# A transformer trunk on one core: the products of probabilities and values with v as the stationary operand, and the probabilities divided on GpSimd

## The chip, the cores and the metric

The kernel runs on one core of a Trainium2 chip. The metric is the device time of one execution in microseconds (us); the median of three runs is compared. Engines are named as in the profile: PE (TensorE's matmuls), PEld (its weight loads), DVE (VectorE), ACT (ScalarE), POOL (GpSimd) and SP, which issues most of the DMAs.

## The reference

Two layers over 256 tokens of width 1024. Each has a mixer, then a feed-forward part: dense (width 2816) in layer 0, eight experts with two chosen per token (width 3584) in layer 1. What the change touches is the mixer's attention and what follows it:

```python
scores = jnp.einsum('bnqkgd,bnskd->bnkgqs', qb, kb).astype(jnp.float32) * (HEAD_DIM ** -0.5)
scores = jnp.where(valid[None, :, None, None], scores, NEG_INF)
m = jnp.maximum(jnp.max(scores, axis=-1, keepdims=True), sink_b)
p = jnp.exp(scores - m)
denom = jnp.sum(p, axis=-1, keepdims=True) + jnp.exp(sink_b - m)
probs = (p / denom).astype(v.dtype)
out = jnp.einsum('bnkgqs,bnskd->bnqkgd', probs, vb)
...
y_att = rmsnorm(window_attention(q, k, v, sink), att_out_g)
y_conv = rmsnorm(short_conv(bg, cg, u, conv_w), conv_out_g)
return jnp.concatenate([y_att, y_conv], axis=-1) @ w_out
```

There are 8 query heads of 64 columns over 2 key/value heads (4 query heads share one), and 512 channels of short convolution.

## The kernel before, in words

Every engine has its own hand-written list of instructions; semaphores order them against each other, and each engine takes its list strictly in order. So the order of the work around the change is the order of the calls in `mixer(layer)`, which stands once for PE, once for ACT and once for DVE.

A float32 weight is multiplied as two parts, `hi` (ACT's rounded copy) and `lo` (DVE's remainder), and so is the activation (`act_hi`, `act_lo`); `three` issues the three products. A "piece" is 128 x 1024 of weights: PE takes 12 matmuls of 512 columns for it. The pieces of a mixer are numbered q 0 to 3, kv 4 and 5, c 6 to 9, u 10 to 13, b 14 to 17, out0 18 to 21, out1 22 to 25. `hi` and `lo` are rings of six pieces, so ACT can turn out piece n only when PE is through with piece n - 6.

Between the pieces PE does the attention for two blocks of 128 queries, t = 0 and t = 1. `scores` writes the scores of eight heads into banks 0 to 3. On DVE `masked_scores` adds the mask and takes the maximum, two heads at a time; on ACT `exps` takes the exponentials of them, into the tile `prob`, with their sums. `turn_probs` (PE) transposes the 16 squares of `prob` into the same four banks, `probT_copy` brings them to SBUF (two banks by ACT, two by DVE), and `values` multiplies: for each head and each half of the keys the 128 x 128 square of transposed probabilities is the stationary operand and 64 columns of v are streamed, 16 matmuls of 64 columns for each t. `attended` on DVE multiplies the result by 1/denominator (`denominators`, `rden`) into the tile `att`. PE then transposes `att` (eight squares), ACT and DVE make `act_hi` and `act_lo` of it, and `out_pieces` multiplies by `w_out`: first the two pieces of the convolution's channels (k = 4 to 7), then the two of the attention's (k = 0 to 3), for each half of the output columns. The sum of the attention's squares comes from ACT (`ss_a`), that of the convolution's from a DVE reduction and a matmul with ones (L2001).

Names in rows and in the order: `raw_d` is the memory in which `prob`, `probT`, qkv, qT, kT and zT lie (it holds the dense part's weights later), `y` and `gated` hold the convolution's result and its squares, `silu` the sums of squares, `raw_gu` the raw weights. SP loads them, and the experts' weights only after the router's decision (`order_done`) at the end of layer 1's mixer.

Of the kernel before, what the change touches and what calls it, by code (L numbers as in the profile page):

```python
# [33 lines left out]
P = 128  # L34
# [26 lines left out]
             ("out0", 4, 1, 2), ("out1", 4, 2, 2)]  # L61
# [269 lines left out]
CONSTS = 7  # L331
# [3 lines left out]
def build_trunk(nc, x_d, pos_d, mix_g, w_in, conv_w, sink, att_g, conv_g, w_out, ffn_g, dg, du, dd,  # L335
                router, eg, eu, ed, final_g, out_d):
    ctx = ExitStack()
    with ctx:
# [8 lines left out]
        def sem(name):  # L347
            return ctx.enter_context(nc.semaphore(name))
# [153 lines left out]
        def e_at(s, g):  # L502
# [21 lines left out]
        att = qT.rearrange("p c n -> p (c n)").rearrange("p (t n) -> p t n", t=NT)  # L524
# [4 lines left out]
        sq_sum = silu[:, 0, :]  # L529

# [22 lines left out]
        av_done, att_done, attss_done, attms_done, attstd_done, attn_done = (  # L553
            sem("av_done"), sem("att_done"), sem("attss_done"), sem("attms_done"), sem("attstd_done"), sem("attn_done"))
# [3 lines left out]
        attT_done, mixhi_done, mixlo_done = sem("attT_done"), sem("mixhi_done"), sem("mixlo_done")  # L558
# [74 lines left out]
        w_out_v = w_out.rearrange("l (h p k) n -> l h p k n", h=2, k=4)  # L633
# [10 lines left out]
        def _(sp):  # L644
# [3 lines left out]
            def mixer_loads(layer):  # L648
# [4 lines left out]
                for name, _, buf, _ in MIX_UNITS:  # L653
# [26 lines left out]
            def dense_down(j):  # L680
                if j < 2:

                    sp.wait_ge(mixlo_done, 8)
                else:
                    sp.wait_ge(lo_done, DENSE_BASE + d_first(2 * (j - 2) + 1, DH) + 2)
# [69 lines left out]
        def _(pool):  # L755
# [13 lines left out]
            nc.gpsimd.dma_start(g_att[:, :, :], att_g.rearrange("l (p k) -> p l k", k=4)).then_inc(consts_in, 16)  # L769
# [28 lines left out]
            nc.gpsimd.dma_start(gain_rows[:, :], ffn_g[1].partition_broadcast(P)).then_inc(gain_in, 16)  # L798
            pool.wait_ge(gain_in, 16)
# [5 lines left out]
        def _(act):  # L805
# [64 lines left out]
            def exps(layer, t):  # L870
# [7 lines left out]
                act.wait_ge(sinkd_done, 2 * layer + t + 1)  # L878
                nc.scalar.activation(esink[:, t, :], sinkd[:, t, :], ACT.Exp).then_inc(exp_done, 1)

            def probT_copy(layer, t):
                act.wait_ge(probT_done, 2 * layer + t + 1)
                for b in range(2):
                    copy(probT[:, b * 512:(b + 1) * 512], bank[b][:, :]).then_inc(probT_out_a, 1)

            def mixer(layer):
# [53 lines left out]
                act.wait_ge(yc_done, layer + 1)  # L940
                for k in range(CT):
                    copy(act_hi[:, 4 + k, :], yc[:, k, :], scale=g_conv[:, layer, k:k + 1]).then_inc(mixhi_done, 1)
# [1541 lines left out]
```

## Time and profile before

| | |
|---|---|
| median of 3 runs | 1271.81 us (1270.8 to 1272.67) |
| profiled execution | 1271.47 us, of it the span 1270.0 us |
| instructions | 31539 |
| PE busy | 1241.2 us (98%) |
| DVE busy | 578.2 us (46%) |
| ACT busy | 435.0 us (34%) |
| POOL busy | 11.8 us (1%) |

"Busy" is the time in which an engine has at least one instruction under way. A row of the timeline gives start, duration, engine, line, what is written and read, the shape, and in brackets how long the engine had sat idle before and what ended it. The difference between the starts of two neighbours on one engine is what the first costs that engine; its duration also has a tail that overlaps the next.

### The profile page before, as it was taken

The page shows a single profiled execution, that of the slowest core. Times are in us where ns is not written, and L with a number is a line of the kernel's source. Part 1 is how long each engine was busy: PE and PEld are TensorE (multiplying, and loading weights), DVE is VectorE, ACT ScalarE, POOL GpSimd, SP SyncE. Part 2 cuts the span into 40 slices and gives each one's busy share as a digit, 9 for nine tenths or more (in the row PEclk, how much of TensorE's full clock was granted, in tenths as well). Part 3 has the DMA queues.
Part 4 walks back from the last instruction along what each step waited for, and adds up shares of the span by engine and source line. Part 5 has one row for each costly group of instructions (what it writes and reads, how often), then busy time and mean ns, then how long its engine had stood idle before and what let it go on. Part 6 is the DMA issues. An engine that isn't in the chain of part 4 may idle for free.

```text
span 1270.0 us, 31539 instructions
## 1 busy us (share of the span) xinstructions
PE 1241.2 (98%) x14347; PEld 967.1 (76%) x14347; DVE 578.2 (46%) x940; ACT 435.0 (34%) x674; POOL 11.8 (1%) x35
## 2 busy tenths in 40 slices
PE   7999999999998999999999999999999999999997
PEld 6888888888887777777767778766677778768894
DVE  5785555556686656565765657421100112210003
ACT  7664444445553544454643445200000000000002
POOL 3000000000000000000000000000000000000000
PEclk9999999999998999999999999999999999999999
DMA  9345844165005999999999999999999999999993
GB/s 344 139 168 208 315 161 172 69 234 195 5 1 205 421 420 425 419 421 421 421 425 421 420 421 421 421 423 419 419 416 420 394 396 396 419 419 421 421 421 134
DMA packets 109018, 419.50 MB, mean 330 GB/s; under 512 B 4632, under 2 KB 8768, under 8 KB 100688
## 3 DMA queue, kind: packets, MB, share of 16 engines
q1 hardware_dynamic: 107776, 416.30, 81.0%
q8 instruction: 115, 1.88, 0.5%
q0 software_dynamic: 544, 1.12, 0.3%
q14 instruction: 23, 0.19, 0.0%
q10 hardware_dynamic: 560, 0.01, 0.0%
HBM read 416.37 MB, written 1.05 MB: 329 GB/s over the span
## 4 chain that ended last, share of the span: by engine, by line
PE 87%; DMA 9%; DVE 2%; ACT 1%; issue 0%; SPq 0%; DVEq 0%
PE bank L2236 26%; PE bank L1854 14%; PE bank L1855 13%; PE bank L1856 13%; PE bank L2300 13%; DMA ring<-in_moe_w_down 5%; DMA ring_after<-in_moe_w_down 2%; DMA ring<-in_moe_w_up 2%; PE bank L2165 2%; PE bank L2171 2%; PE bank L1935 1%; PE bank L1913 1%; PE bank L1925 1%; DMA raw_gu<-in_w_in 1%; ACT w_hi L807 0%; PE bank L2250 0%
## 5 line engine op out<-in xcount | busy, mean ns | idle before, releaser
L1646 DVE TENSOR_TENSOR w_lo<-ring,w_hi 128x896 fp32r<-128x896 f32 (+2 forms) x192 | 202.1, 1088 | 78.8 <-ACT w_hi L807 72.9
L2236 PE MATMUL bank<-ring,late_acts 128*32 128x224 f32 x4736 | 234.0, 353 | 0.0
L2236 PEld LDWEIGHTS bank<-ring,late_acts 128*32 128x32 f32 x4736 | 188.9, 110 | 40.9 <-issue 5.0
L807 ACT ACTIVATE w_hi<-ring 128x896 fp32r<-128x896 f32 (+2 forms) x192 | 176.2, 949 | 115.9 <-PE bank L1856 74.0
L1072 ACT ACTIVATE silu_buf<-bank 128x224 f32<-128x224 f32 (+2 forms) x76 | 29.1, 394 | 433.9 <-PE bank L2236 433.9
L1854 PE MATMUL bank<-hi,act_hi 128*128 128x512 f32 (+1 forms) x400 | 154.6, 387 | 3.6 <-DVE act_lo L1227 1.8
L1856 PE MATMUL bank<-hi,act_lo 128*128 128x512 f32 (+1 forms) x400 | 152.5, 381 | 0.0
L1855 PE MATMUL bank<-lo,act_hi 128*128 128x512 f32 (+1 forms) x400 | 152.5, 381 | 0.0
L1202 DVE TENSOR_TENSOR lo<-raw_gu,hi 128x1024 fp32r<-128x1024 f32 x96 | 113.6, 1221 | 41.2 <-ACT hi L807 41.0
L1669 DVE TENSOR_TENSOR silu_buf<-silu_buf,bank 128x224 f32<-128x224 f32 (+2 forms) x76 | 32.0, 434 | 207.3 <-PE bank L2236 186.0
L807 ACT ACTIVATE hi<-raw_gu 128x1024 fp32r<-128x1024 f32 x96 | 97.5, 1060 | 40.6 <-PE bank L1856 36.8
L2236 PE MATMUL bank<-ring,first_acts 128*32 128x224 f32 x2048 | 104.2, 354 | 0.6 <-ACT silu_buf L1072 0.6
L1854 PE MATMUL bank<-w_hi,wide_hi 128*128 128x512 f32 (+1 forms) x256 | 94.9, 371 | 1.0 <-ACT silu_buf L1072 0.9
L1855 PE MATMUL bank<-w_lo,wide_hi 128*128 128x512 f32 (+1 forms) x256 | 94.0, 367 | 0.0
L1856 PE MATMUL bank<-w_hi,wide_lo 128*128 128x512 f32 (+1 forms) x256 | 93.7, 366 | 0.0
L1854 PEld LDWEIGHTS bank<-hi,act_hi 128*128 128x128 f32 x400 | 75.3, 188 | 19.5 <-issue 3.0
L2236 PEld LDWEIGHTS bank<-ring,first_acts 128*32 128x32 f32 x2048 | 63.6, 110 | 33.0 <-issue 5.1
L2300 PE MATMUL bank<-ring,at_buf 128*32 128x256 f32 x1456 | 85.7, 380 | 1.7 <-DMA ring<-in_moe_w_down 1.7
L1856 PEld LDWEIGHTS bank<-hi,act_lo 128*128 128x128 f32 x400 | 75.2, 188 | 14.8
L1855 PEld LDWEIGHTS bank<-lo,act_hi 128*128 128x128 f32 x400 | 75.3, 188 | 13.8
L2300 PEld LDWEIGHTS bank<-ring,at_buf 128*32 128x32 f32 x1456 | 51.5, 110 | 31.8 <-DMA ring<-in_moe_w_down 3.0
L1854 PEld LDWEIGHTS bank<-w_hi,wide_hi 128*128 128x128 f32 x256 | 48.0, 188 | 11.0 <-DVE w_lo L1646 3.2
(249 smaller groups left out, 1340.2 us busy)
## 6 DMA issues: line engine op xcount, KB each, us to landing
ring<-in_moe_w_up SPq DMA_DIRECT2D x59, 1792.0 KB, 20.3
ring<-in_moe_w_gate SPq DMA_DIRECT2D x58, 1792.0 KB, 20.3
ring<-in_moe_w_down SPq DMA_DIRECT2D x53, 1792.0 KB, 20.4
ring_after<-in_moe_w_down SPq DMA_DIRECT2D x11, 1792.0 KB, 19.7
raw_gu<-in_w_in SPq DMA_DIRECT2D x7, 2048.0 KB, 12.4
raw_gu<-in_dense_w_gate SPq DMA_DIRECT2D x5, 2048.0 KB, 7.8
raw_gu<-in_dense_w_up SPq DMA_DIRECT2D x5, 2048.0 KB, 12.7
raw_d<-in_dense_w_down SPq DMA_DIRECT2D x5, 2048.0 KB, 14.5
```

What stands on the lines that cost most here:

```text
L807: return nc.scalar.activation(out, in_, ACT.Copy, **kw)
L1072: nc.scalar.activation(out, gate, ACT.Silu).then_inc(e_silu_done, 1)
L1202: v.tensor_tensor(out, src, h, ALU.subtract).then_inc(lo_done, 1)
L1646: v.tensor_tensor(w_lo[:, n % WP, 0:b - a], flat(u)[:, a:b], w_hi[:, n % WP, 0:b - a], ALU.subtract).then_inc(w_lo_done, 1)
L1669: v.tensor_tensor(gated_e, gated_e, up, ALU.mult).then_inc(e_gated_done, 1)
L1854: mm(out, ah, wh, start=start, stop=False, **kw)
L1855: mm(out, ah, wl, start=False, stop=False, **kw)
L1856: return mm(out, al, wh, start=False, stop=stop, **kw)
L2165: ins = mm(bank[b][:, i * m:(i + 1) * m], xn[:, t, k * P:(k + 1) * P], sel[:, t, 0:m], start=t == 0, stop=t == 1)
L2171: return mm(bank[b][:, :], gselT[0:m, tile, t * P:(t + 1) * P], yt[0:m, tile, c * 512:(c + 1) * 512], start=start, stop=stop)
L2236: ins = mm(bank[b][32 * c:32 * c + 32, 0:n], acts[STEPS[s][0]][:, k, g.col:g.col + 32], w[:, c], start=k == 0, stop=k == KT - 1)
L2300: ins = mm(bank[g.acc][32 * c:32 * c + 32, g.acc_col:g.acc_col + 256], e_at(s, g)[:, 32 * f:32 * f + 32], flat(u)[:, at:at + 256], start=o ...
```

## The change

In `values` the roles are swapped: 64 columns of v are the stationary operand, and the transposed probabilities of the four heads of one key/value head are streamed, 512 columns at once. The two key/value heads write the two halves of the partitions (0 to 63 and 64 to 127) of the same bank. So the result comes out transposed, with channels on partitions, and PE's eight transposes of `att` are gone, as is the tile. Because 1/denominator now belongs to a column, not to a partition, the probabilities are divided before they are turned: POOL multiplies each head's 128 x 256 probabilities by `rden`, 8 instructions for each t and layer, and `turn_probs` waits for them (`probs_done`). The denominators are made in two batches of four heads, between the masks. `act_hi` and `act_lo` are made straight from the bank of `values`, 128 x 128 at a time for each t; the squares' sums go by DVE and two more matmuls with ones. The channels lie on other partitions, so `w_out`'s attention rows and `g_att` are loaded in another order (three DMAs in the place of two for each half of `w_out`; four small ones in the place of one for `g_att`). For t = 1 ACT copies all four banks of turned probabilities. The turn for t = 0 stands one piece later, and the ones-products one piece later.

```diff
 MIX_UNITS = [("q", 4, 0, 1), ("kv", 2, 1, 1), ("c", 4, 2, 1), ("u", 4, 3, 1), ("b", 4, 0, 1),
-             ("out0", 4, 1, 2), ("out1", 4, 2, 2)]
+             ("out0", 4, 1, 3), ("out1", 4, 2, 3)]
...
-                        for h in range(2):
-                            sp.dma_start(unit[buf][:, 4 * h:4 * h + 4, :],
-                                         w_out_v[layer, h, :, :, c * 512:(c + 1) * 512]).then_inc(unit_in[buf], 16)
+                        cc = slice(c * 512, (c + 1) * 512)
+                        sp.dma_start(unit[buf][:, 4:8, :], w_out_conv[layer, :, :, cc]).then_inc(unit_in[buf], 16)
+                        for g in range(NKV):
+                            sp.dma_start(unit[buf][HD * g:HD * g + HD, 0:4, :], w_out_att[layer, g, :, :, cc])\
+                                .then_inc(unit_in[buf], 16)
...
+            for layer in range(2):
+                for t in range(NT):
+                    for n, b in enumerate(SCORE_BANKS):
+                        if n % 2 == 0:
+                            pool.wait_ge(rden_done, 2 * (2 * layer + t) + n // 2 + 1)
+                        for h in (2 * b, 2 * b + 1):
+                            own = prob[:, h * SEQ:(h + 1) * SEQ]
+                            nc.gpsimd.tensor_scalar(own, own, rden[:, t, h:h + 1], None, ALU.mult).then_inc(probs_done, 1)
...
 # ACT
-                for b in range(2):
+                for b in range(2 if t == 0 else 4):
                     copy(probT[:, b * 512:(b + 1) * 512], bank[b][:, :]).then_inc(probT_out_a, 1)
+
+            def attended(layer, t):
+
+                act.wait_ge(av_done, 2 * layer + t + 1)
+                for k in range(4):
+                    copy(act_hi[:, k, t * P:(t + 1) * P], bank[6 + t][:, k * P:(k + 1) * P], scale=g_att[:, layer, k:k + 1])
+                nc.scalar.activation(prob[:, t * 512:(t + 1) * 512], bank[6 + t][:, :], ACT.Square).then_inc(attss_done, 1)
...
 # DVE
+            def denominators(layer, t, c):
+                i = 2 * (2 * layer + t) + c
+                dve.wait_ge(exp_done, 5 * (i + 1))
+                link(v.tensor_tensor(batch(den, t, c), batch(psums, t, c), batch(esink, t, c), ALU.add))
+                v.reciprocal(batch(rden, t, c), batch(den, t, c)).then_inc(rden_done, 1)
...
+                    if n % 2 == 1:
+                        c = n // 2
+                        dve.wait_ge(masked_done, 4 * i + n + 1)
+                        v.tensor_tensor(batch(sinkd, t, c), batch(sink_sb, layer, c), batch(nmx, t, c),
+                                        ALU.add).then_inc(sinkd_done, 1)
+                    if n >= 2:
+                        denominators(layer, t, n - 2)
...
             def attended(layer, t):
-                dve.wait_ge(av_done, 2 * layer + t + 1)
-                dve.wait_ge(rden_done, 2 * layer + t + 1)
-                v.tensor_tensor(att[:, t, :].rearrange("p (h d) -> p h d", h=NH),
-                                bank[6 + t][:, :].rearrange("p (h d) -> p h d", h=NH),
-                                rden[:, t, :].unsqueeze(2).to_broadcast([P, NH, HD]), ALU.mult).then_inc(att_done, 1)
+
+                i = 2 * layer + t
+                dve.wait_ge(attss_done, i + 1)
+                tt = slice(t * P, (t + 1) * P)
+                for k in range(4):
+                    v.scalar_tensor_tensor(out=act_lo[:, k, tt], in0=bank[6 + t][:, k * P:(k + 1) * P],
+                                           scalar=g_att[:, layer, k:k + 1], in1=act_hi[:, k, tt],
+                                           op0=ALU.mult, op1=ALU.subtract).then_inc(attlo_done, 1)
+                v.tensor_reduce(asq_sum[:, tt], prob[:, t * 512:(t + 1) * 512].rearrange("p (k q) -> p q k", k=4),
+                                AX, ALU.add).then_inc(asq_summed, 1)
...
 # PE
             def turn_probs(layer, t):
 
                 for n, b in enumerate(SCORE_BANKS):
-                    pe.wait_ge(exp_done, (NH + 1) * (2 * layer + t) + 2 * n + 2)
+                    pe.wait_ge(probs_done, NH * (2 * layer + t) + 2 * n + 2)
...
             def values(layer, t):
-                i = 2 * (2 * layer + t + 1)
-                pe.wait_ge(probT_out_a, i)
-                pe.wait_ge(probT_out_v, i)
-                for h in range(NH):
-                    g = AW + KVW + HD * (h // (NH // NKV))
-                    for kt in range(NT):
-                        ins = mm(bank[6 + t][:, h * HD:(h + 1) * HD], probT[:, h * 256 + kt * P:h * 256 + kt * P + P],
-                                 qkv[:, kt, g:g + HD], start=kt == 0, stop=kt == 1)
+                pe.wait_ge(probT_out_a, 6 * layer + (2 if t == 0 else 6))
+                pe.wait_ge(probT_out_v, 2 * (layer + 1))
+                for kt in range(NT):
+                    for g in range(NKV):
+                        c = AW + KVW + HD * g
+                        four = probT[:, 1024 * g:1024 * g + 1024].rearrange("p (h k q) -> p k h q", h=4, k=NT)
+                        ins = mm(bank[6 + t][HD * g:HD * g + HD, :], qkv[:, kt, c:c + HD], four[:, kt],
+                                 start=kt == 0, stop=kt == 1)
                 ins.then_inc(av_done, 1)
...
-                turn_probs(layer, 0)
-                pe.wait_ge(c_out, 2 * (layer + 1))
-                mix_pieces(layer, "b", (4, 5), 0, 2)
+                pe.wait_ge(c_out, 2 * (layer + 1))
+                mix_pieces(layer, "b", (4, 5), 0, 1)
+                turn_probs(layer, 0)
+                mix_pieces(layer, "b", (4, 5), 1, 2)
...
                 values(layer, 1)
-                out_pieces(layer, 0, 0, 1)
-                pe.wait_ge(att_done, 2 * (layer + 1))
-                for k in range(4):
-                    for t in range(NT):
-                        c = (k % 2) * 256 + t * P
-                        ins = tr(bank[k // 2][:, c:c + P], att[:, t, k:AW:4], ident[:, :])
-                ins.then_inc(attT_done, 1)
-                out_pieces(layer, 0, 1, 2)
+                out_pieces(layer, 0, 0, 3)
...
-                for t in range(NT):
-                    ins = mm(bank[CMS][:, t:t + 1], sq_sum[:, t * P:(t + 1) * P], ones[:, 0:1], start=True, stop=True)
+                pe.wait_ge(asq_summed, 2 * (layer + 1))
+                for i, sums in enumerate((sq_sum, asq_sum)):
+                    for t in range(NT):
+                        c = i * NT + t
+                        ins = mm(bank[CMS][:, c:c + 1], sums[:, t * P:(t + 1) * P], ones[:, 0:1], start=True, stop=True)
                 ins.then_inc(cms_done, 1)
-                out_pieces(layer, 0, 2, 4)
+                out_pieces(layer, 0, 3, 4)
```

Two places of the order carry the argument; line numbers of the changed kernel are its own. The first is DVE from the last masks of t = 1 (`mask`, `nmx`) to the weights of out1. Before:

```order
L1292 TENSOR_TENSOR bank<-bank,mask 128x2x128
L1294 TENSOR_REDUCE mx<-bank 128x2
L1295 SCALAR_TENSOR_TENSOR nmx<-mx,nsink 128x2
L1298 TENSOR_TENSOR sinkd<-sink_sb,nmx 128x8
L1355 TENSOR_SCALAR y<-raw_d,cw 128x256 x4
L1359 SCALAR_TENSOR_TENSOR y<-raw_d,cw,y 128x256 x8
L1313 TENSOR_TENSOR raw_d<-bank,rden 128x512
L1308 COPY raw_d<-bank 128x512 x2
L1302 TENSOR_TENSOR den<-psums,esink 128x8
L1303 RECIPROCAL rden<-den 128x8
L1369 TENSOR_TENSOR y<-y,bank 128x512 x2
L1374 SCALAR_TENSOR_TENSOR act_lo<-y,g_conv,act_hi 128x256 x4
```

And the same place of the changed kernel, from the sink term of the last mask:

```order
L1329 TENSOR_TENSOR sinkd<-sink_sb,nmx 128x2x2
L1310 TENSOR_TENSOR den<-psums,esink 128x2x2
L1311 RECIPROCAL rden<-den 128x2x2
L1388 TENSOR_SCALAR y<-raw_d,cw 128x256 x4
L1392 SCALAR_TENSOR_TENSOR y<-raw_d,cw,y 128x256 x8
L1399 TENSOR_TENSOR y<-y,bank 128x512 x2
L1403 SCALAR_TENSOR_TENSOR act_lo<-y,g_conv,act_hi 128x256 x4
L1406 TENSOR_REDUCE silu<-gated 128x256
L1345 SCALAR_TENSOR_TENSOR act_lo<-bank,g_att,act_hi 128x128 x4
L1348 TENSOR_REDUCE silu<-raw_d 128x128
L1345 SCALAR_TENSOR_TENSOR act_lo<-bank,g_att,act_hi 128x128 x4
L1348 TENSOR_REDUCE silu<-raw_d 128x128
```

The denominators moved ahead of the convolution, the product with `rden` and the two copies of turned probabilities are gone, and the attention's `act_lo` and sums of squares follow the convolution's at once.

The second place is ACT after the exponentials of t = 1: the copies of the second gate's bank (`xn`), of turned probabilities (`raw_d`), then `act_hi`. Before:

```order
L807 ACTIVATE xn<-bank,rstd 128x512 x2
L807 ACTIVATE raw_d<-bank 128x512 x2
L807 ACTIVATE act_hi<-y,g_conv 128x256 x4
L943 ACTIVATE gated<-y 128x1024
L944 ACT_TABLE_LOAD
L944 ACTIVATE table_warm<-eps 128x1
L807 ACTIVATE hi<-raw_gu 128x1024 x2
L948 ACTIVATE raw_d,ss_a<-raw_d 128x512 x2
L807 ACTIVATE act_hi<-bank,g_att 128x256 x4
L956 ACTIVATE std_a<-ss_a,eps 128x2
```

And of the changed kernel:

```order
L829 ACTIVATE xn<-bank,rstd 128x512 x2
L829 ACTIVATE raw_d<-bank 128x512 x4
L829 ACTIVATE act_hi<-y,g_conv 128x256 x4
L974 ACTIVATE gated<-y 128x1024
L829 ACTIVATE act_hi<-bank,g_att 128x128 x4
L914 ACTIVATE raw_d<-bank 128x512
L829 ACTIVATE act_hi<-bank,g_att 128x128 x4
L914 ACTIVATE raw_d<-bank 128x512
L977 ACT_TABLE_LOAD
L977 ACTIVATE table_warm<-eps 128x1
```

Four copies of turned probabilities stand where two did, and the attention's `act_hi` and squares moved ahead of the table load and of the weights of out1.

## Rows read from the trace of the kernel before

**Rows 1.** Busy time by stretch: start:end, length, engines, clock, DMA share, GB/s

```profile
0.00:104.00 104.00, 95.76 (x526) 81.61 (x526) 73.80 (x149) 62.73 (x118) 11.29 (x34) 1.00 0.63 233
104.00:288.00 184.00, 183.12 (x832) 151.41 (x831) 99.23 (x113) 89.42 (x119) 0.00 (x0) 1.00 0.48 180
392.00:1270.00 878.00, 861.11 (x12414) 648.88 (x12406) 332.82 (x547) 225.13 (x319) 0.16 (x1) 0.99 0.99 405
```

**Rows 2.** Timeline of PE in layer 0's mixer: start, duration, line, count

```profile
53.50 1.91 PE L1925 MATMUL bank<-ident,raw_d 128*128 128x128 f32 x16
...
69.28 3.68 PE L1935 MATMUL bank<-raw_d 128*128 128x64 f32 x32
72.79 1.92 PE L1925 MATMUL bank<-ident,raw_d 128*128 128x128 f32 x16
74.55 1.12 PE L1976 MATMUL bank<-ident,xn 128*128 128x128 f32 x8
76.18 3.76 PE L1935 MATMUL bank<-raw_d 128*128 128x64 f32 x32 [0.51 <-DVE raw_d L1308]
79.75 0.48 PE L1854 MATMUL bank<-hi,act_hi 128*128 128x512 f32 x1
...
82.59 1.12 PE L1994 MATMUL bank<-ident,raw_d 128*128 128x128 f32 x8
83.47 0.48 PE L1854 MATMUL bank<-hi,act_hi 128*128 128x512 f32 x1
...
86.30 0.50 PE L2001 MATMUL bank<-ones,silu 128*128 128x1 f32 x4
86.66 0.49 PE L1854 MATMUL bank<-hi,act_hi 128*128 128x512 f32 x1
```

**Rows 3.** Timeline of PE in layer 1's mixer, `values` of t = 1

```profile
360.38 3.76 PE L1935 MATMUL bank<-raw_d 128*128 128x64 f32 x32 [0.51 <-DVE raw_d L1308]
```

**Rows 4.** Groups by line and form: busy us, mean ns, idle before

```profile
L2236 PE MATMUL bank<-ring,first_acts 128*32 128x224 f32 x2048 | 104.2, 354 | 0.6 <-ACT silu_buf L1072 0.6
```

**Rows 5.** Timeline of DVE in layer 0's mixer

```profile
47.11 0.43 DVE L1292 TENSOR_TENSOR bank<-bank,mask 128x256 f32<-128x256 f32 x1 [2.05 <-PE bank L1913]
...
56.67 1.28 DVE L1308 COPY raw_d<-bank 128x512 f32<-128x512 f32 x2
57.87 1.40 DVE L1347 SCALAR_TENSOR_TENSOR xn<-bank,rstd,xn 128x512 f32<-128x512 f32 x2
...
59.49 4.58 DVE L1202 TENSOR_TENSOR lo<-raw_gu,hi 128x1024 fp32r<-128x1024 f32 x4
63.99 0.42 DVE L1292 TENSOR_TENSOR bank<-bank,mask 128x256 f32<-128x256 f32 x1
...
69.24 1.14 DVE L1355 TENSOR_SCALAR y<-raw_d,cw 128x256 f32<-128x256 f32 x4
70.41 3.38 DVE L1359 SCALAR_TENSOR_TENSOR y<-raw_d,cw,y 128x256 f32<-128x256 f32 x8
...
80.58 2.02 DVE L1378 TENSOR_REDUCE silu<-gated 128x256 f32<-128x1024 f32 x1
...
85.66 1.66 DVE L1382 SCALAR_TENSOR_TENSOR act_lo<-bank,g_att,act_hi 128x256 fp32r<-128x256 f32 x4 [0.54 <-ACT act_hi L807]
```

**Rows 6.** Timeline of ACT in layer 0

```profile
65.37 0.48 ACT L875 ACTIVATE raw_d<-bank,nmx 128x256 f32<-128x256 f32 x1 [0.30 <-DVE nmx L1295]
...
74.75 1.08 ACT L807 ACTIVATE raw_d<-bank 128x512 f32<-128x512 f32 x2 [3.31 <-PE bank L1925]
...
77.61 1.71 ACT L807 ACTIVATE act_hi<-y,g_conv 128x256 fp32r<-128x256 f32 x4 [1.78 <-DVE y L1369]
79.23 1.04 ACT L943 ACTIVATE gated<-y 128x1024 f32<-128x1024 f32 x1
```

**Rows 7.** Timeline of POOL near the start

```profile
9.05 0.39 POOL L787 TENSOR_SCALAR_AFFINE_SELECT mask<-mask 128x256 f32<-128x256 f32 x1
9.40 1.27 POOL L789 TENSOR_SCALAR_AFFINE_SELECT before<-before 128x128 f32<-128x128 f32 x1
```

More of the change, by code:

```diff
@@ L529, in build_trunk, with batch @@
         sq_sum = silu[:, 0, :]
+        asq_sum = silu[:, 1, :]
+        def batch(a, t, c):
+            return a[:, t, :].rearrange("p (g c i) -> p c g i", g=NKV, c=2)[:, c]
         unit_in = [sem(f"unit_in{n}") for n in range(4)]
@@ L798, in _ @@
             nc.gpsimd.dma_start(gain_rows[:, :], ffn_g[1].partition_broadcast(P)).then_inc(gain_in, 16)
+            for layer in range(2):
+                for t in range(NT):
[5 more added lines that the diff above has]
+                            nc.gpsimd.tensor_scalar(own, own, rden[:, t, h:h + 1], None, ALU.mult).then_inc(probs_done, 1)
             pool.wait_ge(gain_in, 16)
@@ L1341, in mixer @@
                 pieces(16, 18)
-                probT_copy(layer, 0)
+                probT_copy(layer)
                 dve.wait_ge(c_out, 2 * (layer + 1))
@@ L1348, in mixer @@
                                            in1=z[:, t, :], op0=ALU.mult, op1=ALU.mult).then_inc(z_done, 1)
-                denominators(layer, 0)
                 pieces(18, 22)
@@ L1362, in mixer @@
                     link(ins)
-                attended(layer, 0)
-                probT_copy(layer, 1)
-                denominators(layer, 1)
                 dve.wait_ge(bT_done, layer + 1)
@@ L1368, in mixer @@
                     c = slice(2 * b, 2 * b + 2)
[L1369 to L1371 removed]
+                    v.tensor_tensor(yc[:, c, :], yc[:, c, :], bank[4 + b][:, :].rearrange("p (c n) -> p c n", c=2),
+                                    ALU.mult).then_inc(yc_done, 1)
                 for k in range(CT):
[L1373 removed]
+                    dve.wait_ge(mixhi_done, 4 * layer + k + 1)
                     v.scalar_tensor_tensor(out=act_lo[:, 4 + k, :], in0=yc[:, k, :], scalar=g_conv[:, layer, k:k + 1],
                                            in1=act_hi[:, 4 + k, :], op0=ALU.mult, op1=ALU.subtract).then_inc(mixlo_done, 1)
[L1376 removed]
                 dve.wait_ge(sq_done, layer + 1)
                 v.tensor_reduce(sq_sum, sq.rearrange("p k n -> p n k"), AX, ALU.add).then_inc(sq_summed, 1)
+                attended(layer, 0)
+                attended(layer, 1)
                 pieces(22, 24)
[L1380 to L1385 removed]
+                dve.wait_ge(cstd_done, layer + 1)
                 v.reciprocal(rstd_a[:, :], std_a[:, :])
[L1387 removed]
                 v.reciprocal(rstd_c[:, :], std_c[:, :]).then_inc(rstds_done, 1)
@@ L1874, in mix_pieces, with in_done @@
                     ins.then_inc(piece_used, 1)
+            def in_done(layer, k):
+                if k < 4:
+                    pe.wait_ge(attlo_done, 8 * layer + 4 + k + 1)
+                else:
+                    pe.wait_ge(mixlo_done, 4 * layer + k - 3)
             def out_pieces(layer, c, j0, j1):
```

75 lines of the change are left out of this document (28 added, 47 removed).

## The prediction

> **What bounds the kernel now.** I read the busy time by stretch first [rows 1]. In the last 878 us, the experts, the DMA engines are busy 0.99 of the time at 405 GB/s; that stage moves a fixed number of bytes and starts when layer 1's router has decided, so it is as long as before and only starts earlier or later. Ahead of it PE is the bound: 183.1 of 184 us in the dense part, 95.8 of the first 104 us with both mixers alike. So what PE saves or waits for in a mixer arrives at the end one for one, and POOL, nearly idle, costs nothing unless somebody waits for it. The timeline of PE through layer 0's mixer is the second view [rows 2]: rows follow each other without idle time but for 0.51 us ahead of the second `values`. Layer 1 shows the same row 284.2 us later, with the same wait [rows 3], so I work out layer 0 and double. The third view is DVE and ACT beside it [rows 5, 6], because what PE no longer does they still have to feed.
>
> **What PE saves if nothing made it wait.** `values` costs 72.79 - 69.28 = 3.51 us each time [rows 2]. Two matmuls that write different partitions of a bank run side by side in this trace: the experts' matmuls with 32 columns of weights need 104.2 us for 2048 records of 224 columns, 0.051 us each although one lasts 0.354 [rows 4], four at a time. That is 0.051 x 4 / 224 = 0.91 ns a column. A new `values` is 4 matmuls of 512 columns, two records each as these, two side by side: 8 x 512 x 0.91 ns / 2 = 1.9 us. It saves 1.6 us, four times 6.4 us. The eight transposes of `att` cost 83.47 - 82.59 = 0.88 us a layer, gone. The ones-products double, 0.36 us more a layer (86.66 - 86.30), and I take 0.45. With the idle 0.51 us a layer that would be 6.4 + 1.8 - 0.9 + 1.0 = 8.3 us. I do not expect it, for two chains end later than PE.
>
> **Chain one: DVE to `act_lo`.** A piece costs PE 82.59 - 79.75 = 2.84 us, 2.8 behind another piece. The turn of t = 0 moves behind a "b" piece, 53.50 to 56.3; with 1.7 us for the turn (74.55 - 72.79) and 0.2 us to the copier, the copies start at 58.2 instead of 56.67 [rows 2, 5]. The two copies, the two z products and no denominators bring the `lo` pieces to 60.7 (before 59.49) and the second masks to 65.2 (before 63.99). The masks took 69.24 - 63.99 = 5.25 us. Added now: a sink term (0.2), the first denominators (0.3), and after the last maximum a wait for two exponentials with their sums and the sink's (0.48 each [rows 6], about 1.1 with the reading of the sums), then 0.3 for the last denominators, some 1.9 in all. So the convolution starts at 72.4, 3.1 us late, and ends 4.6 later at 77.0. The product with `rden`, the copies and the denominators that followed it are gone, which is why the rest is hardly late. From there: first half of y 0.7, four `act_hi` 1.6, square 1.04 (ACT, to 80.4), the sum of squares on DVE 2.0 (to 82.4; before 80.58 + 2.02 = 82.6) [rows 5, 6]. Then for t = 0 four `act_lo` of half the columns of [rows 5], 0.26 each, and a sum over 512 elements, half of L1378's, 1.0: 84.5. The first `act_lo` of t = 1 lands at 84.9, and the attention's first output piece needs it. That piece started at 86.66. It is 1.75 us earlier, but the ones-products, which were ahead of it, now come behind it with 0.8 us: net 0.95 us a layer. Put otherwise, for no change that piece may start at 85.85.
>
> **Chain two: POOL to `values`.** The last denominators of t = 1 are ready at 72.5. POOL has four products of 128 x 256 to make, p each; no row of before shows one. The nearest rows are a select on POOL over 128 x 256 float32, one input and one output, which cost 9.40 - 9.05 = 0.35 us to the next start, and a select over 128 x 128 that lasted 1.27 [rows 7]. I take p = 0.45, the shape's own row and something for reading a scalar for each partition; ends 0.35 and 1.27. Ready at 74.4, last quarter of the turn 0.4, ACT starts its copies at 75.0 and needs 4 x 0.5 + 0.1 = 2.1 us for four banks (1.08 for two [rows 6]): `values` starts at 77.2, a microsecond later than the 76.18 of before, and ends at 79.1. Behind it come two convolution pieces, 5.6 us, to 84.7. That is inside the 84.9 of chain one. So p is hidden up to 0.5, costs 0.4 us a layer for each 0.1 above it, and at 0.74 the gain is gone. Queued behind the waiting turn are PE's transposes of b, for which DVE's `y` waits, so a long wait pushes chain one as well.
>
> **Other parts.** Turn of t = 0: the masks start at 47.1 [rows 5], so by the same steps the first batch starts at 51.5 and the second at 54.4 (4.4 and 7.3 us after the masks); ready at 54.4 + 4p = 56.2 against the turn's last quarter at 57.5, hidden up to p = 0.75. Its place behind a piece costs nothing on PE, since the same piece is done either way. The `w_out` DMAs move the same bytes; the three more small ones of `g_att` stand on POOL's queue ahead of the mask's select at 9.05 [rows 7] and push it by a few us, while the mask is first used at 47.11 [rows 5]. Weights of out1: ACT has the attention's copies and squares ahead of them, 80.4 + 2 x (4 x 0.25 + 0.5) = 83.4, a table load and two pieces of 1.0, and DVE's 1.1 each (4.58 / 4 [rows 5]) end before 89; PE wants them at 91.3. SP's loads for the dense part wait for the same semaphores in either kernel, shifted by under 2 us, and the dense part is PE's.
>
> **Sum.** 2 x 0.95 = 1.9 us. Against the profiled execution, 1271.5 - 1.9 = 1269.6; that one lies 0.3 us under the median of the runs shown, so 1269.9, say 1270.0. A measurement tells apart about 0.2%, 2.5 us; this is inside.
>
> **Rivals.**
> POOL is slow. At p = 1.0 the eight products of t = 0, from 51.5 in one row, end at 59.5, 2.1 us after the turn wants them, and the eight of t = 1, from 69.6 + 2.1, at 79.7 instead of 74.3: the attention's output pieces start at 84.7 + 5.4 = 90.1, 4.3 us a layer behind the 85.85, 1280.4. In the same way 0.8 gives 1273.9 and 1.27 gives 1289. For it: a select of that length stands in [rows 7]. Against it: its neighbour with twice the columns cost 0.35. It decides from p = 0.74, slower beyond noise from 0.82.
>
> POOL and DVE get in each other's way. Behind the denominators DVE runs eight products with two SBUF inputs, 3.4 us [rows 5], just when POOL makes its last two or three. If POOL could work only between them, its last products come at 77.9, the turn ends at 78.4, four copies at 80.7, `values` at 82.7, the output pieces of the attention at 88.3 instead of 84.9: 2.45 us a layer behind the 85.85, 1276.7. If both merely stretch, DVE by 0.8 us, chain one eats it: 0.15 us gained a layer, 1271.5. No row of before has POOL and DVE at work together after 11 us. The Trainium skill, "SBUF — State Buffer", section "Who interferes with whom", says that a DVE instruction with two SBUF inputs contends with a GpSimd instruction that reads SBUF, and that whoever comes first keeps the shared port pair. By that rule this rival is the case, by the selects' rows alone the forecast is.
>
> Chain one is shorter than I think: if the sum over 512 elements costs 0.7 and the first `act_lo` comes at once, 84.5, and p is under 0.4: 1.35 us a layer, 1269.1; with another 0.3 off the wait for the exponentials, 1268.5. All 8.3 us would need both chains gone: 1263.5; DVE's list speaks against it.
>
> The two halves of `values` do not run side by side (3.5 us again; no row has matmuls of 64 weight columns, and only the 32-column ones prove it): 1.6 us more behind the second turn, 80.7, output pieces at 86.3: 0.45 us a layer worse than before, 1272.7. The same 1.6 us at t = 0 fall into PE's wait for POOL.
>
> **How the numbers follow.** Forecast chain as worked out, 0.36; halves not side by side, 0.05; mild stretch, 0.10: together 0.51 within 0.2%. Chain one shorter by enough to pass 2.5 us in two layers, 0.19, and the full saving 0.02: faster 0.21. POOL slow 0.18, shut out 0.10: slower 0.28. The likeliest case alone spans 1269.0 to 1271.5. The range goes from 1268.0 (the short chain with 0.1 beyond it) to 1278.0, which leaves out p near 1 and the full saving, under 0.2 together.
>
> **What would show it.** `values` at 1.9 us and 16-record transposes of `att` gone; starts of POOL's products 0.35 to 0.5 apart, in both t, also beside DVE's products of the convolution; `values` of t = 1 starting near 77.2 behind a wait of about 1.5 us for ACT; the piece of k = 0 starting near 84.9 behind a short wait for DVE's `act_lo`; out1 at 91.3 instead of 92.2. Wrong if POOL's steps are over 0.7, if the eight DVE products stretch beyond 3.4, or if PE does not wait for `act_lo` at all.

## The result and the profile after

| | before | changed |
|---|---|---|
| median, us | 1271.81 (5 runs, 1270.8 to 1272.7) | 1284.88 (5 runs, 1283.79 to 1285.3) |
| profiled execution, its span | 1271.47, 1270.0 | 1285.3, 1283.5 |
| POOL busy, us | 11.8 | 47.3 |

The ratio is 1.0099, 95% interval [1.0088, 1.0109]: 13.1 us slower, where 1270.0 with a range up to 1278.0 was forecast.

The timeline of PE through layer 0's mixer, as in [rows 2] (the same columns):

```profile
58.30 1.03 PE L1956 MATMUL bank<-ident,raw_d 128*128 128x128 f32 x8
61.23 0.66 PE L1956 MATMUL bank<-ident,raw_d 128*128 128x128 f32 x4 [1.90 <-POOL raw_d L820]
63.04 0.66 PE L1956 MATMUL bank<-ident,raw_d 128*128 128x128 f32 x4 [1.15 <-POOL raw_d L820]
63.45 0.66 PE L1878 MATMUL bank<-hi,act_hi 128*128 128x512 f32 x1
...
67.97 2.00 PE L1944 MATMUL bank<-raw_d 64*128 64x256 f32 x16
...
76.55 1.94 PE L1966 MATMUL bank<-raw_d 128*64 128x512 f32 x8
78.42 1.17 PE L1956 MATMUL bank<-ident,raw_d 128*128 128x128 f32 x8
80.79 0.66 PE L1956 MATMUL bank<-ident,raw_d 128*128 128x128 f32 x4 [1.20 <-POOL raw_d L820]
82.82 0.66 PE L1956 MATMUL bank<-ident,raw_d 128*128 128x128 f32 x4 [1.37 <-POOL raw_d L820]
83.31 1.13 PE L2008 MATMUL bank<-ident,xn 128*128 128x128 f32 x8
85.63 1.94 PE L1966 MATMUL bank<-raw_d 128*64 128x512 f32 x8 [1.19 <-ACT raw_d L829]
87.50 0.50 PE L1878 MATMUL bank<-hi,act_hi 128*128 128x512 f32 x1
```

Where `values` took 3.51 us there, it takes 76.55 to 78.42, 1.87: the two halves do run side by side. But PE, which waited for nothing but 0.51 us, now waits four times for POOL's products (L820), 5.6 us, and once for ACT's four copies. In layer 1 the waits for POOL are longer still (in total, times, the longest):

```profile
PE bank L1956 <- POOL raw_d L820: 7.0, 6, 1.9
```

In layer 0 the turn of t = 0 lasts from 58.30 to 63.45, 5.15 us instead of 1.66; that of t = 1 from 78.42 to 83.31, 4.89 instead of 1.76. What they wait for is in the timeline of POOL, once over its first four products and then over the four that follow:

```profile
53.67 3.65 POOL L820 TENSOR_SCALAR raw_d<-raw_d,rden 128x256 f32<-128x256 f32 x4 [39.38 <-DVE rden L1311]
...
57.30 5.68 POOL L820 TENSOR_SCALAR raw_d<-raw_d,rden 128x256 f32<-128x256 f32 x4
```

Four products take 3.65 us, so p is 0.90, and the next four take 5.68. Over the eight, the view by tile gives the spread (minimum, median, maximum in ns):

```profile
L820 POOL TENSOR_SCALAR raw_d<-raw_d,rden x8: 916/920/2974, 53.7 to 62.1; 128x256 f32<-128x256 f32 x8
```

One product, that of 57.30, takes 2.97 us and ends at 60.3. The timeline of DVE shows what ran beside it, and beside the products of t = 1:

```profile
57.21 2.36 DVE L1225 TENSOR_TENSOR lo<-raw_gu,hi 128x1024 fp32r<-128x1024 f32 x2 [0.57 <-ACT hi L829]
...
78.11 1.84 DVE L1388 TENSOR_SCALAR y<-raw_d,cw 128x256 f32<-128x256 f32 x4
79.99 3.79 DVE L1392 SCALAR_TENSOR_TENSOR y<-raw_d,cw,y 128x256 f32<-128x256 f32 x8
```

The two subtractions of `lo`, both inputs in SBUF, end at 59.57; POOL, which began 0.09 us after the first of them, is through 0.7 us later, most of a product's own 0.90. At t = 1 both engines only stretch: DVE 1.84 us instead of 1.14 and 3.79 instead of 3.38 [rows 5], POOL 0.95 to 1.03 a product.

The last view is the busy time by stretch (columns as in [rows 1], the clock behind the engines), first layer 1's mixer of the kernel before, then the changed kernel:

```profile
288.00:392.00 104.00, 101.22 (x586) 85.17 (x585) 72.38 (x133) 57.73 (x118) 0.37 (x1) 1.00 0.17 61
...
58.00:63.40 5.40, 2.35 (x18) 1.75 (x17) 1.57 (x2) 0.12 (x1) 4.98 (x4) 1.00 0.00 0
63.60:67.00 3.40, 3.40 (x10) 2.64 (x10) 3.27 (x5) 3.27 (x5) 0.00 (x0) 0.50 0.00 0
370.80:377.60 6.80, 5.03 (x18) 3.19 (x20) 4.79 (x12) 3.89 (x9) 1.27 (x2) 0.50 0.00 0
...
415.00:900.00 485.00, 480.55 (x5260) 356.81 (x5262) 269.37 (x361) 201.05 (x255) 0.00 (x0) 1.00 1.02 421
```

Behind the turn of t = 0, in which PE was busy 2.35 of 5.40 us, the granted clock is 0.50, which is the lower of its two levels, for 3.4 us; in layer 1 it is 0.50 for 6.8 us inside and behind the turn of t = 1. The kernel before has neither stretch: its clock is 1.00 over both mixers (the first row here, and [rows 1] for layer 0). The experts' stage moves its bytes at 421 GB/s as before; the loss is all ahead of it. From `scores` of t = 0 to the first work of the dense part, layer 0's mixer takes 110.39 - 48.03 = 62.36 us instead of 103.13 - 45.95 = 57.18, and layer 1's, up to the router's first transposes, 395.88 - 337.37 = 58.51 instead of 381.98 - 330.13 = 51.85: 11.8 us together. The other 1.3 of the 13.1 us lie outside the mixers. Below, L0 and L1 are these two stretches.

### The profile page after: what moved, and what is told of

Its sections match the earlier page's. It is cut to its first block, busy times and chain, and to the rows that moved or that the text cites. A ratio compares the mean times of both kernels' runs of the same rounds, so it can differ in the third digit from the quotient of the medians.

```text
span 1283.5 us, 31399 instructions
## 1 busy us (share of the span) xinstructions
PE 1241.3 (97%) x14243; PEld 957.0 (75%) x14243; DVE 583.7 (45%) x956; ACT 437.5 (34%) x686; POOL 47.3 (4%) x70
## 3 DMA queue, kind: packets, MB, share of 16 engines
q8 instruction: 114, 1.87, 0.5%
## 4 chain that ended last, share of the span: by engine, by line
PE 83%; DMA 7%; DVE 5%; POOL 3%; ACT 1%; issue 1%; SPq 0%; DVEq 0%
PE bank L2264 26%; PE bank L2328 13%; PE bank L1878 13%; PE bank L1880 12%; PE bank L1879 12%; DMA ring<-in_moe_w_down 5%; POOL raw_d L820 3%; DMA ring_after<-in_moe_w_down 2%; PE bank L2193 2%; PE bank L2199 2%; DVE w_lo L1670 1%; DVE lo L1225 1%; DVE mx L1323 1%; DMA raw_gu<-in_w_in 1%; PE bank L2278 0%
```

## The experiments

The kernel before was timed again with each group of runs, 1272.36 us in the first and 1272.13, 1272.19 and 1272.29 in the others, and each ratio is against its own group. The code of each experiment is an excerpt.

**No division.** POOL's products are out, and the turn waits for the exponentials.

```diff
-                        for h in (2 * b, 2 * b + 1):
-                            own = prob[:, h * SEQ:(h + 1) * SEQ]
-                            nc.gpsimd.tensor_scalar(own, own, rden[:, t, h:h + 1], None, ALU.mult).then_inc(probs_done, 1)
...
-                    pe.wait_ge(probs_done, NH * (2 * layer + t) + 2 * n + 2)
+                    pe.wait_ge(exp_done, 10 * (2 * layer + t) + (2, 4, 7, 9)[n])
```

> The changed kernel without POOL's 32 products; the turns of probabilities wait for the exponentials instead, so the probabilities are left undivided. Theory: POOL's steps of 0.90 us (one of 2.97) and the half clock that PE gets after waiting for them are the loss in the mixers; what is left is the 2.1 us lost at the start and the gain of chain one, 0.95 us a layer: 1271.8 + 2.1 - 1.9 = 1272.0. Rival, the swapped products or the extra work on ACT and DVE are slower by themselves: 1278 or more.

The probabilities stay undivided here. Measured 1270.29, ratio 0.9984 [0.9974, 0.9993]; L0 56.19, L1 50.78. So the division is the whole loss, 14.6 us, and the rest of the change gains 0.99 us in layer 0 and 1.07 in layer 1. The router decides on other numbers here, but the time from its first transposes to the end is about the same (888.7 us, before 888.0), so that does not make the gain. PE's waits up to the dense part, by what it waited for (us in total, times, the longest):

```profile
PE bank L1870 <- DVE act_lo L1395: 1.5, 1, 1.5
PE bank L1958 <- ACT raw_d L821: 0.9, 1, 0.9
PE bank L1870 <- DVE act_lo L1337: 0.2, 1, 0.2
```

The large one is for `act_lo` of the convolution (L1395), ahead of the first output piece.

**The small DMAs last.** The first product of PE started at 11.98 us in the changed kernel and at 10.58 before; `g_att`'s four DMAs stand early on POOL's queue. Here they are issued behind `gain_rows`, with no other edit.

```diff
-            for layer in range(2):
-                for g in range(NKV):
-                    nc.gpsimd.dma_start(g_att[HD * g:HD * g + HD, layer, :],
...
             nc.gpsimd.dma_start(gain_rows[:, :], ffn_g[1].partition_broadcast(P)).then_inc(gain_in, 16)
+            for layer in range(2):
+                for g in range(NKV):
+                    nc.gpsimd.dma_start(g_att[HD * g:HD * g + HD, layer, :],
...
```

> The changed kernel with the four small DMAs of g_att issued last on POOL's queue instead of second. Theory: at the start these DMAs hold up the first weights (PE's first product at 11.98 instead of 10.58, then a stretch at half clock), so 2.1 us come back: 1282.8. Rival, the start was late for another reason (w_out's DMAs, a chance of that execution): 1284.9.

1284.7, ratio 1.01 [1.0085, 1.0116]: no gain. PE's first product stood at 10.88 here, but at 10.80 in the run without division too, where the DMAs are early. The late start belonged to one execution. Executions differ there in any case: `scores` of t = 0 starts at 45.95 us in the kernel before, and at 46.72 and 48.12 in two runs below that only add an unused tile to it.

**DVE waits for POOL.** The subtractions that held up a product at t = 0 wait until POOL is through.

```diff
                 masked_scores(layer, 0)
+                dve.wait_ge(probs_done, 2 * NH * layer + NH)
                 pieces(16, 18)
```

> The changed kernel with one more wait: DVE makes the lo pieces 16 and 17 only after POOL's eight products of t = 0. Theory, DVE's subtraction of two SBUF inputs shuts POOL out: the product that lasted 2.97 us lasts 0.9, all steps are 0.90, and the turn of t = 0 ends 2.06 us earlier; DVE pays for it behind, so the whole gains only 0.4 to 1.5 us a layer: 1282 to 1284. Rival, that product is long for a reason of its own (the semaphore wait, a code load): it stays at 2.97 us.

1284.24, ratio 1.0094 [1.0078, 1.0109]. The hold-up is gone, as the timelines of POOL and DVE show:

```profile
52.38 7.24 POOL L820 TENSOR_SCALAR raw_d<-raw_d,rden 128x256 f32<-128x256 f32 x8 [38.98 <-DVE rden L1311]
...
59.65 2.36 DVE L1225 TENSOR_TENSOR lo<-raw_gu,hi 128x1024 fp32r<-128x1024 f32 x2 [4.30 <-POOL raw_d L820]
```

Eight products in 7.24 us, none longer than the others, and PE's turn of t = 0 takes 3.07 us instead of 5.15. But DVE's list is now late by what POOL takes, its masks and denominators of t = 1 with it, and PE waits there: L0 is 63.09, L1 57.75. In layer 0 the low clock has also moved to the turn of t = 1 and behind it, where it lasts longer than the 3.4 us of the changed kernel:

```profile
79.50:85.50 6.00, 4.56 (x19) 3.04 (x19) 3.93 (x9) 2.84 (x6) 1.44 (x2) 0.50 0.35 137
```

The median is 0.6 us below the changed kernel's, inside the intervals: removing the collision in this way buys nothing.

**A product of half the width.**

```diff
-                            own = prob[:, h * SEQ:(h + 1) * SEQ]
+                            own = prob[:, h * SEQ:h * SEQ + P]
```

> The changed kernel, but each of POOL's 32 products covers 128 of a head's 256 keys; the other half of the probabilities stays undivided. Theory: a product's time goes with its columns, so 0.45 to 0.5 us each; that is the price the prediction put in, and the time then is the predicted one, 1270 to 1272, with waits of PE for POOL only at t = 0, where one product is still shut out for two microseconds. Rival: most of 0.90 is a fixed price for each instruction (0.7 or more stays): 1279 or more.

The half divided probabilities change what the router decides, and the program takes another branch behind it (6244.65 us), so only the mixers can be read. The first four products of layer 0:

```profile
52.55 2.36 POOL L820 TENSOR_SCALAR raw_d<-raw_d,rden 128x128 f32<-128x128 f32 x4 [38.95 <-DVE rden L1311]
```

0.58 us from start to start, against 0.90 for 256 columns: 0.26 for the instruction and 0.32 for each 128 columns. Neither theory had that; 0.26 is paid whatever the width. L0 is 59.34, L1 53.80: 3.15 and 3.02 us above the run without division, so even at p = 0.58, with the hold-up at t = 0 still there (one product lasts 2.64 us), the change is 2 us a layer slower than the kernel before. The time of 1270 to 1272 that I expected at this p is refuted too.

**PE's waits filled.** PE repeats transposes while it waits for POOL.

```diff
                 for n, b in enumerate(SCORE_BANKS):
+                    for r in range(((0, 0, 4, 2), (0, 2, 2, 3))[t][n]):
+                        last = SCORE_BANKS[n - 1]
+                        for h in (2 * last, 2 * last + 1):
+                            for kt in range(NT):
+                                c = (h % 2) * 256 + kt * P
+                                tr(bank[last][:, c:c + P], prob[:, h * 256 + kt * P:h * 256 + kt * P + P], ident[:, :])
                     pe.wait_ge(probs_done, NH * (2 * layer + t) + 2 * n + 2)
```

> The changed kernel, but PE repeats the transposes of the quarter before (0.44 us a time, same data into the same place) while it waits for POOL: 4 and 2 times ahead of the third and fourth quarter of t = 0, 2, 2 and 3 times ahead of the second, third and fourth of t = 1. POOL is as slow as before. Theory: the stretches at half clock behind the waits (63.6 for 3.4 us, 370.8 for 6.8 us) go, worth half their length, 5.1 us: 1279.8, or a little over where a repeat ends after POOL. Rival: the low clock comes with something else, or costs nothing: 1285 or more.

1282.93, ratio 1.0084 [1.0071, 1.0097]. Its stretches:

```profile
57.00:62.00 5.00, 4.58 (x41) 4.11 (x40) 1.02 (x1) 0.00 (x0) 4.42 (x4) 1.00 0.00 0
62.00:66.00 4.00, 4.00 (x24) 3.12 (x24) 3.83 (x6) 3.83 (x6) 0.00 (x0) 1.00 0.00 0
...
364.00:375.00 11.00, 8.95 (x64) 6.22 (x60) 8.94 (x22) 6.09 (x16) 6.43 (x7) 1.00 0.00 0
```

With PE kept busy the clock stays at 1.00 in both places, so its fall comes from the waits. But it was worth 1.65 us in the two mixers (1.95 between the medians, whose intervals overlap), not 5.1. In layer 0 PE comes from the turn to the next `scores` 1.6 us earlier (8.09 instead of 9.67 us), and waits that much longer at the next turn, whose start DVE and POOL set: L0 62.31 against 62.36. Only layer 1's part stays, L1 56.91 against 58.51.

**Division split.** POOL divides the first four heads of each t, ACT the last four; the small DMAs are late as above.

```diff
...
# ACT, at the end of exps
+                act.wait_ge(rden_done, 2 * (2 * layer + t) + 2)
+                for b in SCORE_BANKS[2:4]:
+                    for h in (2 * b, 2 * b + 1):
+                        own = prob[:, h * SEQ:(h + 1) * SEQ]
+                        copy(own, own, scale=rden[:, t, h:h + 1]).then_inc(probs_act, 1)
...
```

> POOL divides the first four heads of each t only, ACT the last four (a copy with a scale for each partition, in its list behind the sinks' second exponential); g_att's small DMAs are last on POOL's queue. Theory (the loss is POOL's 0.90 us a product, twice my 0.45, with the stop behind DVE's subtractions and the half clock that PE's waits bring): four products of 0.9 are done 3.6 us after the first denominators, ahead of the turn's first half, and ACT's four of 0.4 us are done 1.7 us after the second; nobody waits, 1270.3 to 1271.0, as without any division. Rival one, the loss lies in whatever the change adds beside POOL: still over 1280. Rival two, ACT is the next bound (its 1.7 us for each t push the copies of turned probabilities, the weights' hi and act_hi): 1273 to 1276.

1274.82, ratio 1.0025 [1.0014, 1.0035]; L0 58.17, L1 52.94. PE's waits in layer 0:

```profile
PE bank L1965 <- POOL raw_d L820: 2.6, 2, 1.4
PE bank L1975 <- ACT raw_d L829: 0.7, 1, 0.7
PE bank L2017 <- ACT xn L829: 0.5, 1, 0.5
PE bank L1883 <- DVE act_lo L1350: 0.2, 1, 0.2
```

At t = 0 nobody waits. At t = 1 the first denominators come when PE already wants the turn, and then four products of 0.9 us are in the way; behind them ACT's division pushes its copies of b and of the turned probabilities (rival two, in part). The split takes back 10 of the 13 us and is still 2.7 slower than before. In its mixers the granted clock falls once, to 0.50 in layer 1, for 3.4 us behind the turn of t = 1.

**DVE's chain alone.** Again nothing is divided; DVE makes the convolution's first four products ahead of the last denominators.

```diff
...
+                    if t == 1 and n == 3:
+                        dve.wait_ge(zT_out, 2 * (layer + 1))
+                        for k in range(CT):
+                            ins = v.tensor_scalar(yc[:, k, :], zT[:, k, 0:SEQ], cw[:, layer, 0, k:k + 1], None, ALU.mult)
+                        link(ins)
                     if n >= 2:
                         denominators(layer, t, n - 2)
...
```

> The changed kernel without any division (the probabilities stay undivided), as in the first experiment, and DVE makes the convolution's first four products ahead of the last denominators of t = 1, in the 0.99 us in which it waits for ACT. Theory: without the division PE's only large wait is 1.55 us a layer for act_lo of the convolution, at the end of DVE's chain; that chain gets 0.9 us shorter, so two layers give 1.8: 1268.5. Rival: ACT's copies, of which PE waited 0.95 us, bind at once: 1270.

1267.72, ratio 0.996 [0.9946, 0.9973]; L0 55.15, L1 49.74, each 1.04 us shorter than without the early products. With the division out of the way DVE's chain is what sets the mixer's end, as the prediction had it.

**Three engines divide.** The whole computation again: at t = 0 DVE takes POOL's second half, at t = 1 POOL three heads and ACT five, with ACT's copies of b between the exponentials, the edit above, and two of the four copies back on DVE.

```diff
...
# ACT, in exps of t = 1
+                        copy(bb[:, n // 2, :], bank[4 + n // 2][:, :], scale=rstd[:, n // 2:n // 2 + 1]).then_inc(b_out, 1)
...
+                        mine = ((2 * SCORE_BANKS[1], 2 * SCORE_BANKS[1] + 1) if n == 2 else (2 * b2 + 1, 2 * b3, 2 * b3 + 1))
...
```

> The whole computation, with the division spread over whoever is idle. t = 0: POOL the first four heads, DVE the last four in its 2.7 us of idle time ahead of the weights of b. t = 1: POOL the first two heads and the fifth, ACT the third and fourth between two exponentials and the last three behind them; ACT's two copies of b go between the exponentials; DVE makes the convolution's first four products ahead of the last denominators, where it waited 1.0 us, and takes two of the four banks of turned probabilities again. Theory: values of t = 1 ends 1.2 us a layer earlier against scores(1) than in the split, DVE's chain no longer binds, 0.2 us a layer are won at t = 0: 1274.8 - 2.8 = 1272.0, within a microsecond of the kernel before. Rival: POOL and DVE beside each other, and ACT's longer list ahead of the exponentials, eat it: 1274 or more.

1275.02, ratio 1.0022 [1.0013, 1.0031]: the rival's time. Rows of POOL, PE and DVE in its layer 0, from the timelines:

```profile
74.60 1.38 POOL L823 TENSOR_SCALAR raw_d<-raw_d,rden 128x256 f32<-128x256 f32 x1 [1.97 <-DVE rden L1322]
...
76.03 1.09 PE L1983 MATMUL bank<-ident,raw_d 128*128 128x128 f32 x8 [2.25 <-POOL raw_d L823]
...
77.23 1.29 DVE L1353 COPY raw_d<-bank 128x512 f32<-128x512 f32 x2 [1.03 <-PE bank L1983]
```

POOL's one late product takes 1.38 us beside DVE's convolution (L1409, which starts at 74.42), PE waits 2.25 us for it, DVE then waits 1.03 us in the middle of its list for PE, and PE pays again for the late `act_lo`.

**Where the tiles lie.** To test the small DMAs in the kernel before, I let them load an unused tile of 32 bytes a partition there, behind `g_att`.

```diff
         g_att = sb("g_att", [P, 2, 4])
+        spare = sb("spare", [P, 2, 4])
...
+                    nc.gpsimd.dma_start(spare[HD * g:HD * g + HD, layer, :],
...
```

> The kernel before, in which the four small DMAs of the changed kernel load a spare tile in the place of g_att's one, and g_att comes last on POOL's queue. Theory, they alone delay the start: 1271.8 + 2.1 = 1273.9, the first product of PE near 12.0. Rival, harmless by themselves: 1271.8.

1296.95, ratio 1.0195 [1.0181, 1.0209], and the start was not late (first product 10.95). The loss was in the experts' stage, which no theory had. Three runs of the kernel before took it apart: the tile without the DMAs, a tile of 64 bytes, and the 32-byte tile with everything behind it moved back, by giving `eps` and `table_warm` one place.

> The kernel before with one tile of 32 bytes a partition that nothing reads or writes, allocated behind g_att, so that everything allocated later lies 32 bytes further on. DMAs as before. Theory (the 24.6 us that the kernel before with the four small DMAs lost in the experts' stage, at 409 instead of 421 GB/s, come from where the tiles lie): about 1297. Rival: they come from the small DMAs or their order: 1272.

> The kernel before with an unused tile of 64 bytes a partition behind g_att, where 32 bytes cost 24.5 us. In the kernel before, the first raw weight tile and the experts' ring begin at a multiple of 512 bytes. If what matters is a multiple of 64: 1272. If it is a multiple of more than 64: 1297 again, or part of it.

> The kernel before with the same unused tile of 32 bytes as in the run that took 1296.7, but two one-element tiles (eps, table_warm) share one place of 32 bytes, so that everything behind the unused tile lies where it lay before, the experts' ring at a multiple of 512 bytes. If the position of the large tiles made the 24.5 us: 1272. If the mere presence of another tile, or the position of the small ones, did: 1297.

They gave 1296.66 us, ratio 1.0192 [1.0177, 1.0207], 1294.26, 1.0165 [1.0149, 1.0181], and 1272.73, 1.0002 [0.9992, 1.0012]. The tile itself and the DMAs cost nothing; the position of the large tiles does. The stretch from 415 to 900 us, first with the tile of 32 bytes:

```profile
415.00:900.00 485.00, 469.96 (x5199) 345.17 (x5201) 258.03 (x343) 191.62 (x239) 0.00 (x0) 1.00 1.02 409
```

and then with the same tile and the rest back in place:

```profile
415.00:900.00 485.00, 479.00 (x5424) 352.39 (x5426) 259.47 (x344) 191.95 (x242) 0.00 (x0) 1.00 1.02 421
```

The DMA engines are as busy in both (1.02) and move 409 instead of 421 GB/s. The changed kernel moves 421, and its large tiles begin where those of the kernel before do, so this is no part of its loss.

## Why the prediction was wrong

**The step that failed** is the price of one POOL product, "I take p = 0.45, the shape's own row and something for reading a scalar for each partition; ends 0.35 and 1.27". It measured 0.90 us, and without these products the loss is gone. The row I went by was a select, another instruction on the same engine and shape. The upper end was misread: the select of 128x128 that lasted 1.27 was not a slow one. It ran from 9.40 to 10.67 beside DVE's subtraction of `lo`, the first row here; the same select takes 0.28 in the run with the small DMAs last, where `lo` starts only at 9.61, the second row:

```profile
9.24 1.28 DVE L1202 TENSOR_TENSOR lo<-raw_gu,hi 128x1024 fp32r<-128x1024 f32 x1 [0.24 <-ACT hi L807]
...
8.70 0.28 POOL L798 TENSOR_SCALAR_AFFINE_SELECT before<-before 128x128 f32<-128x128 f32 x1
```

So the row was a first case of what later held up a product, and that 0.90 lay between the ends I kept was luck. The range left out p near 1, though I allowed up to 1.27. All three signs that the prediction named for being wrong came: POOL's steps over 0.7, DVE's eight products stretched beyond 3.4 (3.79), and PE not waiting for `act_lo`.

**The rival "POOL is slow"** had 0.18. By its numbers (1273.9 at 0.8, 1280.4 at 1.0) p = 0.9 gives about 1277, 2.65 us lost a layer; measured 1284.9, 5.2 us lost in layer 0 and 6.7 in layer 1. The 8 us between, as far as rows can tell:
- POOL shut out, the second rival (0.10), is the case too, but I had it at t = 1 beside the products of the convolution, where both engines merely stretch. It happens at t = 0 beside the two subtractions of `lo`: 2.06 us each time, 4.1 in two layers. The turn of t = 0 hands its lateness on whole. Against the run without division, counted from `scores` of t = 0, it ends 3.49 us later in layer 0, and the first denominators of t = 1 come 3.49 us later too. Here they are without division (`scores` at 46.90) and in the changed kernel (`scores` at 48.03), with POOL's eight products that follow:

```profile
70.35 0.18 DVE L1303 RECIPROCAL rden<-den 128x4 f32<-128x4 f32 x1
...
74.97 0.18 DVE L1311 RECIPROCAL rden<-den 128x4 f32<-128x4 f32 x1
...
75.25 7.52 POOL L820 TENSOR_SCALAR raw_d<-raw_d,rden 128x256 f32<-128x256 f32 x8 [12.26 <-DVE rden L1311]
```

The run of half width agrees: both come 1.35 us later. So at p = 0.58, which my slope of 0.4 us a layer for each 0.1 above 0.5 calls nearly free, the mixers were still 2.2 and 2.0 us slower than before. No run takes the hold-up away by itself; where DVE waited instead, its own lateness took the place of it. The two rivals hold together, and I priced them one by one. The Trainium skill, "SBUF — State Buffer", section "Who interferes with whom", says that a DVE instruction with two SBUF inputs contends with a reading GpSimd instruction and that the holder keeps the shared port pair. The trace agrees for the subtractions (one product 2.97 us instead of 0.92); for the convolution's products, with two SBUF inputs as well, it shows 0.95 to 1.03, so the rule does not tell the size. I had weighed it against the selects' rows and looked for both engines at work only after 11 us, past the one row that shows it.
- The clock: 1.65 us, by the run with filled waits, nearly all of it in layer 1. No part of the prediction had it, and the doubling of layer 0 could not show it.
- POOL's stretch beside the convolution at t = 1: 7.52 us for eight products instead of 7.2, 0.3 a layer.
- Outside the mixers: 1.3 us, not taken apart. The profiled execution started 2.1 us late, and executions differ in that.

These are differences between rows, added up as if each arrived at the end (4.1 + 1.65 + 0.6 + 1.3 = 7.7); no run isolates the first or the third.

**Chain one held.** Without the division the change gains 0.99 and 1.07 us a layer where 0.95 was forecast, and shortening DVE's list by 1.0 us moved the end by 1.04. Its last link was placed one step off: in the run without division PE waits 1.54 us for the convolution's `act_lo` ahead of the first output piece, and only 0.25 ahead of the attention's, where I looked for all of it. In the changed kernel PE comes too late to wait for either.

**Terms of the sum:** `values` 1.9 forecast, 1.87; four copies by ACT 2.1, 2.07; sum over 512 elements 1.0, 1.07; `act_lo` of half the columns 0.26, 0.28; ones-products 0.8, 0.81. Durations read from the same instruction in another size held; the one taken from another instruction did not. The nearest version of the whole computation is still 2.7 us slower than the kernel before; the idea is worth 4.5 us only if the division costs nobody anything, as in the run that leaves it out and so computes something else.

## What to carry to other kernels

Before work moves to an idle engine, time one instruction of that kind on it, look at what ran beside the row that you take a price from, and put that price where its result is wanted at once: POOL had 1200 us to spare here and lost 14.6, since eight products take 7.2 us and the turn is wanted 4.7 us (t = 0) and 1.7 us (t = 1) behind its first denominators, as the run without division shows. Where an engine gets a new wait, price what the wait does next as well: the other engines' lists that shift, and the low clock behind it. And look at the positions of the tiles beside the order of the instructions: an unused tile of 32 bytes cost almost twice what the whole change did.

## What the runs showed of the hardware

- A POOL product with a scalar for each partition, float32 in SBUF: 0.90 us for 128x256, 0.58 for 128x128, from start to start. Four of 128x256 take POOL 3.65 us, ACT 1.71 (split run) and DVE 1.30 (three-engine run, from their timelines).
- Large tiles 32 or 64 bytes behind a multiple of 512 cost 24.5 and 22.1 us in 880 us of transfers at full DMA load. The Trainium skill, "DMA: Bandwidth & Descriptors", section "How a descriptor splits into AXI transactions", says that a transaction must start at a 256-byte boundary, so that a descriptor which starts elsewhere begins with a partly used one. It says this of what a transaction reads; here it is the tiles written to that moved. The runs agree in direction: equal busy share, 3% less moved. No run tells 256 from 512.
- PE's granted clock fell to 0.50 behind layer 0's turn of t = 0, in which PE waited 3.05 of 5.15 us, and not behind the same turn of layer 1, with waits of 1.87 and 1.15 us; there it fell at t = 1. When repeated transposes filled the waits it stayed at 1.00 in every turn. What tells the two turns apart I did not find.
